# One program for the projection, the GLA and the neighbourhood heads, with a pair's blocks and jobs in the order 0 to 4

## The reference

```python
x = layer_norm(x, ln_in_g, ln_in_b)
proj = x @ w_in[l]
gq, gk, gv, gg, glr, nq, nk, nv = jnp.split(proj, pts, axis=-1)
o_gla = gla_mixer(gq, gk, gv, gg, glr, ...)                    # 4 heads, gated linear attention, forward and backward
o_na = neighbourhood_attention(nq, nk, nv, na_rpb[l])          # 8 heads of 64, window 8 x 16 on a grid 64 wide
mix = jnp.concatenate([o_gla, o_na], axis=-1) @ w_out[l]
x = layer_norm(DEEPNORM_ALPHA * x + mix, ln1_g[l], ln1_b[l])
f = conv_gated_mlp(x, w_up[l], conv_w[l], conv_b[l], w_down[l])
x = layer_norm(DEEPNORM_ALPHA * x + f, ln2_g[l], ln2_b[l])
```

## Time and profile before

| | us |
|---|---|
| median of 3 runs | 3387.92 |
| lowest, highest | 3386.04, 3389.48 |
| the profiled execution | 3386.37 |
| its span | 3384.1 |
| PE busy | 3177.5 |
| DVE busy | 1744.9 |
| ACT busy | 1105.5 |
| POOL busy | 372.8 |

### The profile page before, as it was taken

One profiled execution on the slowest core, in us unless ns is written; L12 is line 12 of the kernel. 1 busy time (PEld: TensorE's weight loads), 2 busy tenths in 40 slices (PEclk: granted clock), 3 DMA queues, 4 the chain that ended last, 5 costly groups with the idle time before them and its releaser, 6 DMA issues.

```text
span 3384.1 us, 42316 instructions
## 1 busy us (share of the span) xinstructions
PE 3177.5 (94%) x15664; PEld 2548.7 (75%) x15664; DVE 1744.9 (52%) x3389; ACT 1105.5 (33%) x2118; POOL 372.8 (11%) x374
## 2 busy tenths in 40 slices
PE   6998998885999995999999999999999999999997
PEld 4776766664777774788888888888888888888885
DVE  6647646742666663555645335353353533543377
ACT  2346245421443441444333222132222222222222
POOL 0012100004333400000003000030000200020000
PEclk9999999987999998899999999999999999999998
DMA  7799697848777738788787556575565755656553
GB/s 265 298 301 277 232 289 243 285 150 240 252 227 254 252 141 324 282 308 290 254 317 288 199 188 235 198 287 197 190 234 197 289 195 193 233 202 236 193 197 114
DMA packets 267883, 807.95 MB, mean 239 GB/s; under 512 B 44706, under 2 KB 111138, under 8 KB 220320
## 3 DMA queue, kind: packets, MB, share of 16 engines
q1 hardware_dynamic: 234784, 608.11, 52.6%
q10 hardware_dynamic: 21312, 155.20, 12.8%
q0 software_dynamic: 11584, 41.95, 3.3%
HBM read 622.04 MB, written 187.24 MB: 239 GB/s over the span
## 4 chain that ended last, share of the span: by engine, by line
PE 58%; DVE 2%; DMA 2%; ACT 0%; issue 0%; SPq 0%; POOL 0%; DVEq 0%; ACTq 0%
PE trunk_ps_h L76 12%; PE trunk_ps_h L77 12%; PE trunk_ps_h L78 12%; PE trunk_ps_f L76 7%; PE trunk_ps_f L78 7%; PE trunk_ps_f L77 7%; DMA trunk_raw<-in_w_out 1%; DMA trunk_raw<-in_w_down 1%; PE trunk_ps_h L2016 0%; DVE trunk_w L1758 0%; DVE trunk_y L1777 0%; DVE trunk_stats L1781 0%; ACT trunk_w L1675 0%; DVE trunk_y L1814 0%; DVE trunk_y L1816 0%
## 5 line engine op out<-in xcount | busy, mean ns | idle before, releaser
L76 PE MATMUL trunk_ps_h<-trunk_xt,trunk_w 128*128 128x512 f32 x1760 | 685.7, 390 | 1.4 <-DVE trunk_xt L1822 1.4
L77 PE MATMUL trunk_ps_h<-trunk_xt,trunk_w 128*128 128x512 f32 x1760 | 685.4, 389 | 0.0
L78 PE MATMUL trunk_ps_h<-trunk_xt,trunk_w 128*128 128x512 f32 x1760 | 685.4, 389 | 0.0
L1852 DVE SCALAR_TENSOR_TENSOR trunk_tt<-trunk_hb,trunk_cw,trunk_tt 128x512 f32<-128x512 f32 x220 | 187.0, 850 | 678.2 <-ACT trunk_tt L1701 678.2
L76 PE MATMUL trunk_ps_f<-trunk_w,trunk_m 128*128 128x512 f32 x1168 | 456.9, 391 | 20.6 <-DMA trunk_m<-mix_lo 19.3
L78 PE MATMUL trunk_ps_f<-trunk_w,trunk_m 128*128 128x512 f32 x1168 | 455.1, 390 | 0.0
L77 PE MATMUL trunk_ps_f<-trunk_w,trunk_m 128*128 128x512 f32 x1168 | 455.0, 390 | 0.0
L1699 ACT ACTIVATE trunk_hb<-trunk_ps_h 128x512 f32<-128x512 f32 x220 | 131.7, 599 | 885.9 <-PE trunk_ps_h L78 885.9
L76 PEld LDWEIGHTS trunk_ps_h<-trunk_xt,trunk_w 128*128 128x128 f32 x1760 | 330.9, 188 | 70.7 <-DVE trunk_xt L1822 1.8
L78 PEld LDWEIGHTS trunk_ps_h<-trunk_xt,trunk_w 128*128 128x128 f32 x1760 | 330.8, 188 | 68.9
L77 PEld LDWEIGHTS trunk_ps_h<-trunk_xt,trunk_w 128*128 128x128 f32 x1760 | 330.9, 188 | 68.5
(11 more groups left out here) (204 smaller groups left out, 4472.5 us busy)
## 6 DMA issues: line engine op xcount, KB each, us to landing
trunk_w<-wu_s SPq DMA_DIRECT2D x88, 1024.0 KB, 4.8
trunk_w<-wu_s ACTq DMA_DIRECT2D x88, 1024.0 KB, 4.8
near_xr<-xt_s SPq DMA_DIRECT2D x160, 512.0 KB, 5.8
front_xr<-xt_s SPq DMA_DIRECT2D x120, 512.0 KB, 6.3
wu_s<-trunk_w SPq DMA_DIRECT2D x44, 1024.0 KB, 4.8
trunk_w<-wd_s SPq DMA_DIRECT2D x44, 1024.0 KB, 4.8
trunk_w<-wd_s ACTq DMA_DIRECT2D x44, 1024.0 KB, 4.8
trunk_raw<-in_w_up SPq DMA_DIRECT2D x44, 512.0 KB, 5.8
```

Source lines behind the costliest of these rows:

```text
L76: pe.matmul(out, lh, rh, start=first, stop=False, skip_group_check=skip)
L77: pe.matmul(out, lh, rl, start=False, stop=False, skip_group_check=skip)
L78: return pe.matmul(out, ll, rh, start=False, stop=last, skip_group_check=skip)
L1852: dve.scalar_tensor_tensor(out, hb[:, i, s, a_j:a_j + BLK], tap[:, a_j:a_j + 1], out, ALU.mult, ALU.add).then_inc(conv_step, 1)
```

## The change

The two programs become one, `attention`, with 320 dense steps and one queue per engine.

- Passes 4 to 7 are the pairs, steps 160 to 319, blocks and jobs in the order 0 to 4. The slice ring has 6 places and loads go 5 steps ahead for all of them.
- From step 160 on the pieces of the GLA outputs lie twice as far apart (`shifted`): the last five outputs have their scores at 161, 167, 173, 179 and 185 and end at step 202.
- Jobs start at `JOBS_AT`: pair 0 at 194 and pair 1 at 225 with 1.5 steps between two, pairs 2 and 3 at 258 and 298 with 2.
- The weights' ring has 8 places instead of 10 (12 in `natten`). The values of a pair lie in the part of it that pairs don't use, in six groups of 16 DMAs for every pair; the first pair's stand at steps 176, 178, ... 186. Buffers of the GLA heads are used again for queries, keys, tables and weights of the jobs, so `make_tables`, `evict_pair`, `add_bias` and others wait once for the end of the heads.
- The 16 copies of the padded bias (`copy_bias`) stand one pass earlier, and the first `load_bias` at step 156.

```diff
-        return [s + by for s in steps]
+        return [s + by if s + by < NSTEP else NSTEP + 2 * (s + by - NSTEP) + 1 for s in steps]
...
-ORDER = (1, 2, 3, 4, 0)
-JOB_AT, JOB_GAP = 18, 2
-N_WRING, N_XRING, N_AHEAD, N_S = 12, 8, 6, 4
+JOBS_AT = [194 + 3 * i // 2 for i in range(JOBS)] + [225 + 3 * i // 2 for i in range(JOBS)] \
+    + [258 + 2 * i for i in range(JOBS)] + [298 + 2 * i for i in range(JOBS)]
...
-GROUPS_AFTER = ((2, 3, 4), (3, 5, 8), (5, 7, 12), (7, 10, 16), (0, 2, 20))
+GROUPS_AFTER = ((0, 2, 4), (2, 3, 8), (3, 5, 12), (5, 7, 16), (7, V_SLOTS, 20), (V_SLOTS, NKG, 20))
...
-XRING, WRING, RAWS, TILES = 6, 10, 3, 8
+XRING, WRING, RAWS, TILES = 6, KC, 3, 8
...
-            return (p - 1) * PER_PASS + PER_PASS - KC - 1 + kc if p else kc - TURN_AHEAD
+            return p * PER_PASS - KC + 1 + kc if p else kc - TURN_AHEAD
...
+                if VG23 * PER_PASS <= n < NV * PER_PASS and n % 2 == 0 and n % PER_PASS < 4 * ROWS_U:
+                    copy_bias(*divmod(n % PER_PASS // 2, 2))
+                if n == NSTEP - 4:
+                    load_masks()
+                    load_bias(0)
+                for i, (_, _, after) in enumerate(GROUPS_AFTER):
+                    if n == JOBS_AT[0] - 18 + 2 * i:
+                        load_nv(0, i)
+                    for p in range(1, PAIRS):
+                        if n == JOBS_AT[(p - 1) * JOBS + after - 1] + 9:
+                            load_nv(p, i)
+                for p in range(1, PAIRS):
+                    if n == JOBS_AT[p * JOBS] - 30:
+                        load_bias(p)
...
+            def job_scores(j):
+                p, u, cb = jobs[j]
+                first, groups, _, _ = UNITS_NA[u]
+                if j == 0:
+                    pe.wait_ge(a_masked, NOUT)
+                pe.wait_ge(nqk_lo, 2 * (p * NBLK + LAST_BLOCK[u] + 1))
+                need(pe, biased, 2 * j)
```

More of the change, by code:

```diff
@@ L462, in _ @@
                     load_lr(i)
-                for i in at(in_step, n):
+                for i in at(logit_at, n):
                     load_qk(i)
@@ L505, in _ @@
                     scale_keys(i)
+                if n == NSTEP + 1:
+                    for p in range(PAIRS):
+                        make_tables(p)
         @block.scalar
@@ L651, in _ @@
                     squares(j)
+                if NSTEP <= n < DENSE and n % KC == KC - 1:
+                    evict_pair(n)
+                for j in job_at(n, 8):
+                    if jobs[j][2] == NQB - 1:
+                        no_out_hi(j)
+                for j in job_at(n, 6):
+                    copy_turned(j)
+                for j in job_at(n, 2):
+                    exps(j)
         @block.vector
@@ new lines, in job_scores @@
+            def job_scores(j):
+                p, u, cb = jobs[j]
+                first, groups, _, _ = UNITS_NA[u]
+                if j == 0:
+                    pe.wait_ge(a_masked, NOUT)
+                pe.wait_ge(nqk_lo, 2 * (p * NBLK + LAST_BLOCK[u] + 1))
+                need(pe, biased, 2 * j)
+                for i, (a, b) in enumerate(((0, 0), (0, 1), (1, 0))):
+                    for side in range(2):
+                        keys = nk[half_of(side), b, first * KG * GRID_W:(first + groups) * KG * GRID_W]
+                        keys = keys.rearrange("p (r c) -> p r c", c=GRID_W)[:, :, BAND_AT[cb]:BAND_AT[cb] + BAND]
+                        mm = pe.matmul(ps_s[side][:, :groups * P], nq[half_of(side), a, u, cb * P:(cb + 1) * P], keys,
+                                       start=i == 0, stop=i == 2)
+                mm.then_inc(s_done, 1)
@@ new lines, in weigh_values @@
+            def weigh_values(j):
+                p, u, cb = jobs[j]
+                first, groups, _, _ = UNITS_NA[u]
+                if j == 0:
+                    pe.wait_ge(o_lo, NOUT)
+                pe.wait_ge(pt_act, j + 1)
+                pe.wait_ge(pt_dve, j + 1)
+                if cb == 0:
+                    need(pe, no_lo, unit_no(j))
+                    for i, (g0, g1, _) in enumerate(GROUPS_AFTER):
+                        if g0 < first + groups and first < g1:
+                            pe.wait_ge(nv_in[i], 16 * NQB * KG * (p + 1))
+                for g in range(first, first + groups):
+                    for side in range(2):
+                        mm = pe.matmul(ps_no[half_of(side), cb * P:(cb + 1) * P], nv(g, g + 1, cb)[:, 0, half_of(side)],
+                                       pt[:, j % 2, side, (g - first) * P:(g - first + 1) * P], start=g == first,
+                                       stop=g == first + groups - 1)
+                mm.then_inc(pv_done, 1)
```

703 lines of the change are left out of this document (317 added, 386 removed).

## The result

The changed kernel takes 3458.9 us (median of 4 runs, 3453.68 to 3462.27) against 3386.98 before: a ratio of 1.021, with a 95% interval of 1.0193 to 1.0228. That is 72 us slower. The forecast was slower, by 25.5, with 3442 as the top of the range: the sign is right, the size is about a third of what was measured.

What follows compares the result with a forecast made beforehand. PE was taken as the bound behind the seam, with some 52 us idle at the seam. The terms, 8.5 - 22 + 27 + 8 + 8 - 4 = +25.5 us on 3386.4, gave 3412 us, range 3370 to 3442.

Steps and rivals of the forecast that it cites:

- term 5: Job stage: a pair's last two value groups fall on one SP step, slices late at 262 and 305: +8 us.
- term 2: Dense steps: 16 more done before the jobs start, at 1.36 us each: -22 us.
- term 1: Seam: SP's queue holds up slices, so first scores start at about 856 us against 847.45: +8.5 us.
- The front: Before the seam: the smaller weights' ring costs 0; bias copies one pass earlier cost 0, with +-5 us.
- Term 3: Tight gaps between jobs of pairs 0 and 1: scores wait for DVE's bias additions: +27 us, bounds 5 and 60.
- Term 4: Tight gaps: block evictions at steps 207 and 247 cost 3 us each, two weight splits 1 each: +8 us.
- the small waits: Half of the old job stage's small waits go: -4 us.
- the tail: Last jobs, bound by DVE: some 5 us longer, PE's stage before about as much shorter: 0, +-5 us.
- A: Seam: loads not held up, first scores at about 805, -42 us there, total 3361; chance 0.16.
- B: Job stage: tight gaps cost little because DVE works earlier, no change, 3377 to 3389; chance 0.12.
- C: Seam: PE keeps the low clock through the whole stretch, slower still, 3434; chance 0.10.

Runs made afterwards that it cites:

- both seam edits: Changed kernel with the loads of outputs 16 to 19 issued later and the first pair's values at every fifth step, nothing else: 3414.5 us, ratio 1.0084.
- The separate groups alone: Changed kernel with only the last value group of a pair issued four steps later, so that no two stand together: 3445.8 us, ratio 1.0173.
- the one with all edits: Changed kernel with additions first on DVE, output loads late, first pair's values every fifth step, weight splits last, last value group four steps later: 3356.9 us, ratio 0.9909.

## Why the prediction was right in sign and short in size

Three terms carry the miss: term 5 left out the weight loads that stand behind SP's other DMAs (28 us), term 2 left out the clock (16 us), and term 1 took the rounds at the seam too short (11 us).

**The front** (forecast 0, +-5): 10 us shorter, not forecast. Before, PE waited 6.8 us at 324 us for a load of the low-rank gates, with a lower clock behind it; after it waits 1.7. With the same 3340 matmuls PE's busy time there is 8.7 us less (636.9 before, 628.2 after), so most of the gain is clock. What in the change did this was not tried.

**Term 1** (first scores at 856 us): the first scores came when forecast (856.8) by luck: two errors cancelled. The mechanism was as described: slices waited for at steps 162, 165, 171, 177 and 183 and from there on. But counted from step 160 the stretch took 152.4 us where the forecast had 141.5: a round is 21 to 26 us where 20 to 22 were taken, and slice 162 came at 723.8 where 737 was said (10 us of this are the front's; the bias loads took 5.8 us, not 8 to 9), but from it to slice 171 there are two rounds (40 us) where the working leaves 24. The six groups went as forecast (7.3 to 8.2 us each, the last issued at 847.5 where 846 was said). So the term is +19 us, not +8.5, and the front's gain hid it. With both seam edits the first scores come 54 us earlier, so the whole term can be taken away, and more.

**Term 2** (-22): 16 steps ahead were done; PE's busy time in the job stage fell by only 9.8 us where 26 should have gone, so the clock took some 16 us back. The clock was left out of the sum without a reason, and this is the second step that failed. The rows show where it falls. Of eleven score waits of 1.0 to 1.7 us in this stage, ten are followed by matmuls at the higher of the two levels; behind each wait of 2.35 us or more there are rows at the lower one, at once or some matmuls later. Six score matmuls at 512 keys take 0.97 us behind a wait of 1.7 and 1.65 behind one of 4.3:

```profile
936.21 0.97 PE L1242 MATMUL front_bank<-front_nk,front_nq 64*128 64x512 f32 x6 [1.69 <-DVE front_mx L1061]
...
1084.12 1.65 PE L1242 MATMUL front_bank<-front_nk,front_nq 64*128 64x512 f32 x6 [4.31 <-DVE front_mx L1061]
```

So the clock is lost mostly behind the long waits, those for weights, slices and evictions, and less behind the forecast's short ones. In the piece of pairs 2 and 3 where the gaps are gone it is back (79.8 of 80 us busy, clock 1.00).

**Term 3** (+27 in 18 gaps, 1 to 2 us each): 23 score waits less four long ones (5.2, 5.4, 10.4 and 4.3) are 19 with 27.4 us, and eight of them lie between 1.4 and 1.7. The mechanism is right: taking the cause away on DVE or in the spacing removed them. That the total is met to the microsecond is in part luck: the gaps at 512 keys are 1.6 to 1.7 where 1.9 was worked out, those beside a table build longer. The Trainium skill (SBUF — State Buffer, "Who interferes with whom") was used for a wait of 3.4 us under a table build. The longest there were 3.2 (at 1044.5, with weight splits of up to 1.1 us and a scaling pair of 1.43) and 2.8 (at 963.7, with a scaling pair of 2.23 us); with POOL issuing DMAs as well it was far worse than the pairs of before (8.3 us), so the rule's direction agrees and the size depends on what else POOL does.

**Term 4** (+8): the waits at the evictions of steps 207 and 247 are 5.4 and 4.3 us where 3 each was said. Splits are within the 27.4 above, so terms 3 and 4 are to be read together: 37 us measured, 35 forecast.

**Term 5** (+8) is the first and largest step that failed. It counted what slices lose behind 32 value DMAs and wrote "at 231 almost nothing". The slices cost 7.0 and 5.6 us, near the 4 each that were said. At 231 it was 10.4 us, because the weight loads of the next pair stand on SP too, with only three buffers, and their splits stand ahead of the jobs' work on ACT and DVE. The same path made the score wait of 5.2 us at 864, behind the weights that followed the first pair's values, the 4.5 us for an eviction that stood on ACT and DVE behind a split, and the 3.8 us at 1178. Together 36.5 us where 8 were counted, before the clock that long waits cost. The separate groups alone gave 13 us back.

**Sum.** Against the net +25.5: the seam 11 more, the clock 16 more, SP's late loads 28 more, terms 3 and 4 in this stage 1 more, the small waits 3 (they fell by 1 and not by 4), the tail 1, the front 10 less: +75.5, for 76 measured between the spans. Of the 4.8 us that the last jobs and the trunk took longer some 4 are the 44 matmuls moved there, as the forecast had it for the tail. The sum divides two profiles of one execution each; the experiments bear out its large terms, but not to the microsecond.

**The rivals.** A (loads not held up, first scores near 805) did not come by itself, but the run with both seam edits starts at 803, and the one with all edits is at 3357 where A had 3361. B fell: the tight gaps cost what term 3 says. C (3434, low clock through the seam) is nearer in size for another reason: the clock in the seam stretch was 0.78 (0.73 before), and most of the loss, 62 of 76 us, was in the job stage. The Trainium skill (TensorE: Matmul & The Clock Gate, Part 1) has the throttled state as the default and sustained activity as what lifts it; the rows agree in direction (0.92 with 77 us of gaps, 1.00 where PE is full).

## What to carry over

An in-order queue that feeds several consumers has one budget: before moving work onto it, list every load that stands behind each block of DMAs and each wait, with the number of buffers it has, not only the loads one is thinking of. An engine named in a wait may itself be waiting for a weight or a slice, so follow it upward to the DMA before changing its order. When two jobs come closer together, put first on each engine what the next job waits for; here that one reordering gave back 35 of 72 us.

## What was not expected of the hardware

- Issuing 16 value DMAs from POOL's queue takes it 8.0 to 8.6 us, where SP takes 7.3 to 8.8, and while POOL issues them and then adds tables, a pair of DVE's SBUF-to-SBUF scalings takes 6 to 12 us, seven times in that run (0.75 at 384 keys with POOL at rest, and up to 2.8 under tables alone). Additions that read PSUM kept their 0.55 us. Why tables behind DMAs hold DVE so much longer than tables alone is open.
- Waits of 2.35 to 3.2 us were already followed by matmuls at the lower clock level (rows at 963.7, 1047.3 and 1102.4), while those of 1.0 to 1.7 us passed almost all without. With 77 us of waits of all sizes the stage's mean granted clock is 0.92 against 0.99, and of the 88 us by which it is longer than the 369 it should have had (394.5 less 26), some 16 are clock.
